# Preparing the second expert phase's first group during the first phase's last groups

## What is computed

```python
idx = i1 * N_KEYS + i2                     # 8 heads x 16 experts per token
gate = jax.nn.softmax(cv, axis=-1)
act = jax.nn.gelu(jnp.einsum('bhkd,bd->bhk', u_emb[idx], xb).astype(jnp.float32), approximate=False)
return jnp.einsum('bhk,bhkd->bd', (gate * act).astype(v_emb.dtype), v_emb[idx])
```

## Time and profile before

| what | value |
|---|---|
| median of 3 runs | 2418.63 us (2416.98 to 2431.54) |
| the profiled execution | 2413.2 us, its span 2411.1 us |
| TensorE busy | 2197.0 us, 91% of the span |
| VectorE, ScalarE, GpSimd busy | 1531.7, 719.1, 394.3 us |
| first expert phase | about 989.8 to 1713.5 us |
| second expert phase | 1757.5 to about 2382.6 us |

### The profile page before, as it was taken

How to read it: one execution, slowest core, us unless ns; L and a number is a source line. 1 busy time by engine, 2 the same in 40 slices (tenths; PEclk the granted TensorE clock), 3 DMA queues, 4 the chain that set the end, 5 groups by cost and what they waited for, 6 DMA issues and landing times.

```text
span 2411.1 us, 34896 instructions
## 1 busy us (share of the span) xinstructions
PE 2197.0 (91%) x14115; PEld 1800.9 (75%) x14115; DVE 1531.7 (64%) x2738; ACT 719.1 (30%) x875; POOL 394.3 (16%) x346
## 2 busy tenths in 40 slices
PE   5999997777679999899999999999489999999995
PEld 2545565665565477788988989988379999999995
DVE  1113355564652278897888888888477676666674
ACT  1212233232220200233454454454222222222221
POOL 3000000000000000003222222223133333333330
PEclk8999997686688999999999999999789999999998
DMA  5111110000201311246787787787788888888872
GB/s 174 64 42 43 48 38 4 2 7 1 76 7 45 135 36 70 93 172 243 260 302 281 261 303 282 259 301 280 286 307 301 308 311 309 312 313 314 313 255 96
DMA packets 164275, 437.33 MB, mean 181 GB/s; under 512 B 11968, under 2 KB 77248, under 8 KB 153792
## 3 DMA queue, kind: packets, MB, share of 16 engines
q1 hardware_dynamic: 116064, 242.81, 28.9%
q0 software_dynamic: 36864, 134.23, 15.3%
q10 hardware_dynamic: 11232, 58.73, 5.9%
HBM read 368.57 MB, written 67.17 MB: 181 GB/s over the span
## 4 chain that ended last, share of the span: by engine, by line
PE 78%; DVE 15%; issue 2%; ACT 2%; DMA 2%; POOL 0%; DVEq 0%; ACTq 0%; SPq 0%
PE bank L1462 26%; PE bank L1404 24%; PE bank L966 9%; PE bank L1413 3%; PE bank L1331 3%; PE bank L967 2%; PE bank L963 1%; DVE sc L1942 1%; DVE si L1941 1%; DVE si L1944 1%; DVE sv L1940 1%; PE bank L1037 1%; DVE sv L1943 1%; DMA act_scratch<-actb 1%; PE bank L1164 1%
## 5 line engine op out<-in xcount | busy, mean ns | idle before, releaser
L1462 PE MATMUL bank<-w_hi,v_hi 128*128 128x448 f32 x1024 | 375.1, 366 | 44.0 <-DVE w_lo L2195 44.0
L1404 PE MATMUL bank<-xhi,u_hi 128*128 128x448 f32 x1024 | 386.7, 378 | 9.1 <-DVE u_lo L1949 8.5
L1404 PE MATMUL bank<-xhi,u_lo 128*128 128x448 f32 x1024 | 376.0, 367 | 0.0
L1404 PE MATMUL bank<-xlo,u_hi 128*128 128x448 f32 x1024 | 375.1, 366 | 0.0
L1462 PE MATMUL bank<-w_lo,v_hi 128*128 128x448 f32 x1024 | 374.8, 366 | 0.0
L1462 PE MATMUL bank<-w_hi,v_lo 128*128 128x448 f32 x1024 | 374.8, 366 | 0.0
L561 POOL DMA_INDIRECT sca<-in_pu_rows,pick x128 | 177.7, 1388 | 739.1 <-DVE sdot L1955 448.3
L2201 DVE TENSOR_TENSOR v_lo<-wring,v_hi 128x4096 fp32r<-128x4096 f32 x32 | 141.6, 4425 | 205.9 <-ACT v_hi L919 205.9
L561 POOL DMA_INDIRECT rows_v<-in_pv,pick x128 | 194.3, 1518 | 463.7 <-DVE xs L2177 388.5
L919 ACT ACTIVATE v_hi<-wring 128x4096 fp32r<-128x4096 f32 x32 | 116.0, 3626 | 458.5 <-PE bank L1462 431.4
L1462 PEld LDWEIGHTS bank<-w_hi,v_hi 128*128 128x128 f32 x1024 | 193.0, 188 | 59.5 <-issue 44.2
(11 more groups left out here) (483 smaller groups left out, 3249.3 us busy)
## 6 DMA issues: line engine op xcount, KB each, us to landing
u_raw<-in_pu SPq DMA_DIRECT2D x64, 1024.0 KB, 4.9
wring<-in_pv SPq DMA_DIRECT2D x32, 2048.0 KB, 16.9
act_scratch<-actb ACTq DMA_DIRECT2D x64, 448.0 KB, 5.8
gate_scratch<-gst ACTq DMA_DIRECT2D x14, 2048.0 KB, 6.7
wts<-act_scratch SPq DMA_DIRECT2D x32, 896.0 KB, 4.7
gring<-gate_scratch SPq DMA_DIRECT2D x32, 896.0 KB, 8.6
wbuf<-in_w_in SPq DMA_DIRECT2D x4, 2048.0 KB, 10.1
wring<-in_w_q SPq DMA_DIRECT2D x4, 2048.0 KB, 8.7
```

The lines of the kernel that those rows point to most:

```text
L1404: ins = mm(bank[b][:, 0:DS], lhsT, rhs[:, 0:DS], **on)
L1462: ins = mm(bank[c][:, 0:DS], lhsT, rhs[:, q, e, :], **on)
```

## The change

The third gated stage gets 13 groups instead of 16 for its 32 quads, so three of its groups (the 3rd, 7th and 13th) have four quads; the last gated stage keeps 4 groups of four quads; three groups, 61 to 63, have no quads (`TAIL`). The sample dots are dealt anew: 70 in the first two stages, 23 in the third, 12 in the last, and five (`TAIL_DOTS`) in each of the three tail groups. Routing in `between` ends two steps earlier: positions at step 8, find_places and place_keys together at step 9, sum_keys at 10, norm_gates at 11. A group's `split_u` follows its second quad, its dots and `between` its last.

The second phase's buffers lie over memory that is free at different times: slot 0's values behind the gather buffers, in scratch of the routing; slot 1's values over `u_raw` (v_raw1) and `u_lo` (v_hi1), v_lo1 over `u_hi`, slot 1's acts and gates over `xhi`, the rest over stage buffers, `gst` among them. So the loads of group 0 are issued one by one in the first phase: values when the last routing is transposed, acts after the last quad, gates when the last gate store has landed; group 1's values when the last u_lo is written. Acts and gates of group 1 wait for the last act store. The load of `gain` moves behind them; in later groups acts and gates are still loaded before values.

ScalarE runs v_hi of group 0 behind group 62's act store, and w_hi of group 0 between the two Gelus of group 63. VectorE runs, in the tail: split_u(62), five dots, split_u(63), five dots, v_lo(0), weights(0), w_lo(0), five dots. Then it waits for all dots and ScalarE's Gelu of them. GpSimd's v gathers wait for the 128 dots. The wait of TensorE and VectorE for each other between the phases is gone. `x1_late` and `sq_late`, used at the very end, move with v_raw. The loop of TensorE over the third gated stage is written out as straight code.

Cut to its core:

```diff
-GROUPS_OF = [0, 16, 16, 16, 4]
+GROUPS_OF = [0, 16, 16, 13, 4]
+TAIL = 3
 G0 = [HEAD0 + sum(GROUPS_OF[:t]) for t in range(5)]
-assert G0[4] + GROUPS_OF[4] == UG
-HEAD_DOTS = 8
-DOTS = [3 if j in (8, 14, 15) else 2 for j in range(16)]
-DOT0 = [HEAD_DOTS + sum(DOTS) * t for t in range(4)]
-assert DOT0[3] + 15 == HEADS * TOPK
+GATED_END = G0[4] + GROUPS_OF[4]
+assert GATED_END + TAIL == UG
+QUADS = [2] * 32 + [4 if j in (2, 6, 12) else 2 for j in range(13)] + [4] * 4
+QUAD0 = [sum(QUADS[:j]) for j in range(len(QUADS) + 1)]
+assert QUAD0[-1] == DS // 4
+HEAD_DOTS, TAIL_DOTS = 8, 5
+DOTS = [3 if j % 16 in (8, 14, 15) else 2 for j in range(32)] + [1 if q == 4 else 2 for q in QUADS[32:45]] + [3] * 4
+DOT0 = [HEAD_DOTS + sum(DOTS[:j]) for j in range(len(DOTS) + 1)]
+assert DOT0[-1] + TAIL_DOTS * TAIL == HEADS * TOPK
...
+        slot1 = ExitStack()
+        v_raw1 = sb("v_raw1", [128, GE * D], scope=slot1)
+        v_hi1 = sb("v_hi1", [128, GE * D], f32r, scope=slot1)
+        slot1.close()
...
+        v_lo1 = sb("v_lo1", [128, GE * D], f32r, scope=second)
+        wts1 = sb("wts1", [128, GE, DS], scope=second)
+        gring1 = sb("gring1", [128, NCH, GE, GC], scope=second)
+        w_hi1 = sb("w_hi1", [128, GE, DS], f32r, scope=second)
+        sb("gap2", [128, 768], scope=second)
+        v_lo0 = sb("v_lo0", [128, GE * D], f32r, scope=second)
+        w_lo0 = sb("w_lo0", [128, GE, DS], f32r, scope=second)
+        w_lo1 = sb("w_lo1", [128, GE, DS], f32r, scope=second)
+        sb("gap3", [128, 512], scope=second)
+        wts0 = sb("wts0", [128, GE, DS], scope=second)
+        gring0 = sb("gring0", [128, NCH, GE, GC], scope=second)
+        w_hi0 = sb("w_hi0", [128, GE, DS], f32r, scope=second)
+        sb("gap4", [128, 448], scope=second)
         rows_v = sb("rows_v", [128, RING, D], scope=second)
+        v_raw0 = sb("v_raw0", [128, GE * D], scope=second)
+        v_hi0 = sb("v_hi0", [128, GE * D], f32r, scope=second)
...
+            def load_values(q, v_src):
+                sp.dma_start(v_raw[q][:, :].rearrange("p (e d) -> p e d", e=GE), v_src).then_inc(s_v[q], 16)
+
+            def load_acts(q, a_src):
+                sp.dma_start(wts[q][:, :, :].rearrange("p e n -> p (e n)"), a_src).then_inc(s_grp[q], 16)
+
+            def load_gates(q, g_src):
+                sp.dma_start(gring[q][:, :, :, :].rearrange("p c e t -> p c (e t)"), g_src).then_inc(s_grp[q], 16)
+
+            sp.wait_ge(S("routed"), 5)
+            sp.wait_ge(S("hk_done"), 4)
+            load_values(0, pv_g[0])
+            sp.wait_ge(S("gmat_done"), DS // 4)
+            for q in range(2):
+                sp.wait_ge(s_act[q], 16 * 2)
+            load_acts(0, act_d[0])
+            for q in range(2):
+                sp.wait_ge(s_gst[q], 16 * (NCH // 2 + 1))
+            load_gates(0, gate_v[0])
+            for q in range(2):
+                sp.wait_ge(S(f"u_lo_ready{q}"), UG // 2)
+            load_values(1, pv_g[1])
             sp.wait_ge(S("dots_done"), 2 * GU + GU * UG)
-            sp.wait_ge(S("gmat_done"), DS // 4)
-            sp.wait_ge(S("xf_ready"), 5)
-            sp.dma_start(gain[:, :], gfin_d.partition_broadcast(128)).then_inc(s_x1, 16)
             for q in range(2):
                 sp.wait_ge(s_act[q], 16 * (UG // 2 + 1))
-                sp.wait_ge(s_gst[q], 16 * (NCH // 2 + 1))
-
-            def load_group(q, v_src, a_src, g_src):
-                sp.dma_start(wts[:, q, :, :].rearrange("p e n -> p (e n)"), a_src).then_inc(s_grp[q], 16)
-                sp.dma_start(gring[:, q, :, :, :].rearrange("p c e t -> p c (e t)"), g_src).then_inc(s_grp[q], 16)
-                sp.dma_start(v_raw[:, q, :].rearrange("p (e d) -> p e d", e=GE), v_src).then_inc(s_v[q], 16)
-
-            pv_g = pv.rearrange("(g e p) d -> g p e d", e=GE, p=128)
-            gate_v = gate_d.rearrange("c p (g e) t -> g p c (e t)", e=GE)
-            for q in range(2):
-                load_group(q, pv_g[q], act_d[q], gate_v[q])
+            load_acts(1, act_d[1])
+            load_gates(1, gate_v[1])
...
-            pool.wait_ge(S("sum_banks_free"), 4)
+            pool.wait_ge(S("row_used"), SLOTS)
...
+            for g in range(HEAD0, GATED_END):
+                split_u(g + 1)
+                first_q, last_q = QUAD0[g - HEAD0], QUAD0[g - HEAD0 + 1]
+                half = (last_q - first_q) // 2
+                for e in range(GU):
+                    gelu_tile(g, e)
+                    for quad in range(first_q + half * e, first_q + half * e + half):
+                        copy_quad(quad)
+                store_acts(g)
+                for pos in range(2, 5):
+                    if g == G0[pos - 1] + 8:
+                        shift_exp(pos, ORDER[pos])
+
+            def high_values(i, g):
+                act.wait_ge(s_v[g % 2], i * 16 + 16 * (g // 2 + 1))
+                act.activation(v_hi[g % 2][:, :], v_raw[g % 2][:, :], ACT.Copy).then_inc(S("v_hi_ready"), 1)
+
+            def high_weights(i, g):
+                act.wait_ge(S("weights_ready"), i * 2 + (g + 1))
+                act.activation(w_hi[g % 2][:, :, :], wts[g % 2][:, :, :], ACT.Copy).then_inc(S("w_hi_ready"), 1)
+
+            for g in range(GATED_END, UG):
                 if g + 1 < UG:
                     split_u(g + 1)
-                for e in range(GU):
-                    gelu_tile(g, e)
-                    if g < G0[4]:
-                        copy_quad(2 * (g - HEAD0) + e)
-                    else:
-                        for r in range(2):
-                            copy_quad(96 + 4 * (g - G0[4]) + 2 * e + r)
+                gelu_tile(g, 0)
+                if g + 1 == UG:
+                    high_weights(0, 0)
+                gelu_tile(g, 1)
                 store_acts(g)
-                if g - 8 in G0[1:4]:
-                    pos = G0[1:4].index(g - 8) + 2
-                    shift_exp(pos, ORDER[pos])
+                if g + 2 == UG:
+                    high_values(0, 0)
+            act.wait_ge(S("dots_done"), 2 * GU + GU * UG)
+            high_values(0, 1)
...
+            high_weights(0, 1)
+            with act.Fori(0, EG // 2 - 1) as i:
+                for g in range(2, 4):
+                    act.wait_ge(S("sum_done"), i * 16 + 8 * (g + 1))
+                    high_values(i, g)
+                    high_weights(i, g)
...
+            for g in range(GATED_END, UG):
+                for e in range(GU):
+                    dots(0, 8, g, e)
 
             pe.sem_inc(S("sum_done"), 2 * KD)
             pe.wait_ge(S("dot_banks_free"), GU * UG + 2)
             pe.wait_ge(S("gmat_copied"), DS // 4 + 2)
-            pe.wait_ge(S("sum_banks_free"), 8)
...
-                split_u(G0[pos] + j + 1)
-                for r in range(sum(DOTS[:j]), sum(DOTS[:j + 1])):
-                    sample_dot(DOT0[pos - 1] + r)
                 after = ORDER[pos + 1]
                 if j == 0:
                     candidates(after)
@@ -1967,15 +2016,14 @@
                     best_pairs(after, j)
                 if j == 7:
                     shift_gates(pos + 1, after)
+                if j == 8:
+                    positions(after)
                 if j == 9:
-                    positions(after)
+                    find_places(after)
+                    place_keys(after)
                 if j == 10:
-                    find_places(after)
+                    sum_keys(after)
...
-                    if pos < 4 and k % 2:
-                        between(pos, k // 2)
-                    if pos == 4:
-                        if k % 4 == 1 and G0[4] + k // 4 + 1 < UG:
-                            split_u(G0[4] + k // 4 + 1)
-                        if k < 15:
-                            sample_dot(DOT0[3] + k)
+                    if quad + 1 - QUAD0[j] == 2:
+                        split_u(HEAD0 + j + 1)
+                    if quad + 1 == QUAD0[j + 1]:
+                        for r in range(DOT0[j], DOT0[j + 1]):
+                            sample_dot(r)
+                        if pos < 4:
+                            between(pos, j - (G0[pos] - HEAD0))
+                        j += 1
...
-            dve.wait_ge(S("dots_done"), 2 * GU + GU * UG)
-            dve.wait_ge(S("row_used"), SLOTS)
-            dve.sem_inc(S("sum_banks_free"), 8)
-            dve.wait_ge(S("sample_acts"), 1)
-            link(TT(sdot[:, :], sdot[:, :], gate[:, 4, :], ALU.mult))
...
+            def tail_dots(g):
+
+                for r in range(TAIL_DOTS):
+                    sample_dot(DOT0[-1] + TAIL_DOTS * (g - GATED_END) + r)
+
+            for g in range(GATED_END, UG - 1):
+                split_u(g + 1)
+                tail_dots(g)
+            dve.wait_ge(s_gst[0], 16 * (NCH // 2 + 1))
             split_v(0)
             weights(0)
             split_weights(0)
+            tail_dots(UG - 1)
+            dve.wait_ge(S("row_used"), SLOTS)
+            dve.wait_ge(S("sample_acts"), 1)
+            link(TT(sdot[:, :], sdot[:, :], gate[:, 4, :], ALU.mult))
```

(37 more changed lines are left out.)

43 lines of the change are left out of this document (17 added, 26 removed).

## The result

The changed kernel took 2395.69 us in the median of 4 runs (2392.25 to 2399.16), the kernel before 2417.81 on the same chip (4 runs, 2415.51 to 2431.54): ratio 0.9897, 95% interval 0.9856 to 0.9938. The time lies inside the forecast range (2379 to 2407), 4.7 us above the forecast of 2391. The saving of 22.1 us is 0.9%; of the three classes of outcome that the prediction weighed it is "within one per cent", which had 0.36, and not "over it", which had 0.60. The profiled execution took 2393.31 us (span 2391.5) by 2413.2 before.

What follows compares the result with a forecast made beforehand. Bound: TensorE's 44.0 us wait before the second phase, a serial chain of loads and preparation. -46.2 - 2.0 + 10.5 + 5.3 + 4.4 = -28.0 from 2413.2 gives 2385.2; plus 5.4 for the median, 2391 us; range 2379 to 2407.

Steps and rivals of the forecast that it cites:

- The chain: Between last quad and group 1, gathers landing one after another through four buffers were to set TensorE's waits.
- G1 = 7.4, G2 = 8.0, G3 = 6.0, G4 = 9.0: Issue-to-landing us of four gathers: fifth dots of groups 61, 62, the five dots behind w_lo(0), and second row of rows_v.
- B5: Fifth dot of tail group 61; its gather was to land in 7.4 us, so u_lo(63) would cause no wait.
- D5: Fifth of the dots behind w_lo(0); its gather was to land in 6.0 us, with little else moving.
- Rival 2: Tail gathers land as slowly as in the second phase, median 11.0 us; saved 14.3, time 2404; chance 0.25.
- 10.5 + 5.3 + 0: TensorE idle us before the second phase's first sums, before group 1, and for u_lo(63).
- 4G - 14.55: TensorE's two gaps together in us, with one landing time G for all four gathers, while each gap binds.
- Gated groups, "-2.0": Last two gated stages: 231.7 us against 233.7, by removing waits on VectorE in the last; bounds 0 and -2.6.
- rival 4: VectorE becomes the bound in the 13-group stage, with partial waits of 1 to 3 us; 2393; chance 0.04.
- The clock, "4.4": TensorE products at half clock after each of two new gaps, 2.2 us lost each; bounds 1.5 and 4.4.
- -28.0: Forecast total change in us: old gap and stage waits removed, two new gaps and clock losses added.
- The rule weighed: VectorE's port lock delays GpSimd's issue of four critical gathers, 4 to 12 us in all; nothing added to the forecast.

Runs made afterwards that it cites:

- e3: Changed kernel with groups 1 and 2 prepared before the fifteenth dot, the row adds and ScalarE's Gelu of the dots; 2387.13 us.
- e4: Changed kernel with groups 0, 1 and 2 prepared between small batches of dots, last Gelu and adds after them; 2377.72 us.
- e5: Changed kernel with six buffers in place of four for the last 16 rows of the sampled dots; 2391.99 us.
- e9: Repeat of e5 (six buffers for the last 16 dot rows), beside a repeat of the changed kernel at 2399.06; 2387.42 us.
- e1: Changed kernel with group 0's loads and group 1's values issued only after all first-phase products; 2411.26 us.
- e6: Changed kernel loading 256 KB instead of 2 MB for each of values 0 and 1, splits rereading those columns; one execution, 2406.31 us.
- e7: e4 with group 0's gates loaded in two parts, the last 64 KB after the last store; 2376.57 us.

## Why the prediction was right, and where its steps failed

**The chain.** Right in kind: four landings in series, in the places named (fifth dot of groups 61, 62 and 63, second row of rows_v), the first wait of 8 to 15 us, a second behind it, nothing else last. Of the signs given, the second wait of 3 to 9 us was 11.6, and the third wait, for u_lo(63), was not among them. e3 and e4 each move a part of that series out of TensorE's way, and each shows the wait belonging to it gone; e5 and e9 shorten the series, and the waits on w_lo shrink from 21.8 to 7.5 and 9.9.

**"G1 = 7.4, G2 = 8.0, G3 = 6.0, G4 = 9.0."** This is the step that failed: the term was mis-sized. The landings were 12.4, 9.2, 11.6 and 9.7, 43.0 for 30.4. The argument for B5 ("issued some 6 us later, when part of that has drained") was wrong: the queues carried 395 GB/s over the 30 us behind the last quad. For D5 "little else moves" was wrong too: SyncE issued acts and gates 1 and gain at 1725.5 to 1727.3 and group 2's loads from 1729.4 on, and the DMA share in 1730 to 1740 is 1.02. I had called those loads hidden; for TensorE they were. That they lengthened the two landings beside them is argued from the DMA share; no run held them back. Rival 2, with 11.0 each, had the size: 44.0 in sum. Its time was 2404; the profiled execution of before less the change's own 13 to 14 us is 2399 to 2401.

**The waits.** Forecast 10.5 + 5.3 + 0, measured 10.2 + 11.6 + 4.3. The formula held: u_lo(63) was to wait if G1 > 8.2, and 12.4 - 8.2 = 4.2. That wait soaked up most of what would have come in the first gap, so 10.5 came out right by two errors. The formula 4G - 14.55 gives 28.5 with the measured sum; TensorE waited 26.1, and 2.2 us in which it ran at the lower clock behind the u_lo wait took the place of waiting.

**Gated groups, "-2.0".** The 13-group stage took 152.2 us by 150.8 (transposes at 1475.0 and 1627.2) and the last gated stage 51.3 as worked out; 20 groups came to 233.1 by 231.7, so -0.6 from the 233.7 that I started from. (That figure counts from 1479.8; the stage's transposes start at 1479.3.) VectorE was busy for 132.2 us in the 13-group stage, by the 132.5 forecast. In the two stages before, TensorE waited 1.1 us for hot_a, which I had not looked at, and they took 2.5 us longer in all; the rest of that is not explained. No wait in the last gated stage beyond 0.5, no u_lo wait in the 13-group stage: rival 4 didn't happen.

**The clock, "4.4".** Three drops in place of two. Behind the three waits 12, 7 and 10 products start 0.37 us apart in place of 0.20 (1702.48 to 1707.13, 1724.85 to 1727.60, 1757.80 to 1761.70), which costs 2.2, 1.3 and 1.9 us: 5.4 together by 4.4. The shortest wait cost the most.

**The sum.** Forecast -28.0. The waits add 10.3, the stages 1.4 and 2.5, the clock 1.0: -12.8, by -12.6 from first dot product to last sum in the two traces. The medians of 22.1 and 17.1 stand closer to 28 than this; a start 7 us earlier in the one execution is what the profile shows of why. So by the traces the mechanism gave 13 to 14 us, half of the sum's 28, and the time came out close to the forecast partly by luck: by the scatter of code that the change doesn't touch.

**The rule weighed.** The gather issued beside v_lo(0), which ran from 1714.34 to 1718.68, took GpSimd 4.88 us, by 0.94 for several others; the one at 1751.75, beside v_lo(1), took 4.88 again:

```profile
1711.98 0.94 POOL L595 DMA_INDIRECT sca<-in_pu_rows,pick  x1 [3.09 <-DVE sdot L2007]
1714.61 4.88 POOL L595 DMA_INDIRECT sca<-in_pu_rows,pick  x1 [1.70 <-DVE sdot L2007]
...
1726.02 1.68 POOL L595 DMA_INDIRECT sca<-in_pu_rows,pick  x1 [6.53 <-DVE sdot L2007]
```

The Trainium skill, page "SBUF — State Buffer", section "SBUF: two separate sides", says that the two engines exclude each other on a port pair; the trace agrees in sign. That gather was not on the chain. The four that were took 0.94, 1.68, 1.68 and 1.05 to issue, 1.6 us above four times 0.94, so the rule explains little of the missing 12.6 us.

## What to carry to other kernels

When loads move beside other work, ask which transfers with few buffers run beside them: a series of landings through a short ring sets the end, each at the length of full queues, not at the median of a quieter stretch. The order of the consumer's work then decides who pays; putting each group's preparation between small batches of ring work, with ScalarE's order and the row adds moved to fit, gave 24 us more than the change did (by the yardstick). And before a few us are read from two profiles, compare stretches that neither kernel changed.

## What the hardware showed that I had not expected

- The same products at the same granted clock (1.00, so 2.4 GHz) come every 202 or 205.8 ns in different executions of one kernel: 2% of the stage, 12 us of the time. Three of the kernels other than the changed one (e1, e5, e6) had the long period too. Its cause is open.
- A gather of half a megabyte took 8.9 to 13.3 us to land on the chains of the changed kernel, with four in flight (median of that stretch 9.9), and 13.5 in the median with six; with 3.5 MB less of other traffic it still took 7.8 to 10.4. In the quieter last 112 us of the first phase before, also with four buffers, the median was 6.0.
- A load can be issued early and gain nothing: 832 KB of gates issued 14 us ahead of the last 64 KB (e7) went with it: of 1792 packets 78 had moved when the last part was issued, and the wait was 5.9 us by 6.1.
- Behind a wait of 4.3 us as many as 12 products ran at 1.2 GHz, behind one of 10.2 us only 7.
